# The right half of the expert outputs goes to a table in DRAM by accumulating indirect DMA, the left half stays with put products, and the up product uses two banks

## The reference: an attention layer, then a mixture of experts

```
scores = sigmoid(t @ w_router);  top 8 of 64 experts per token, gates g
for each block (expert e, up to 128 of its tokens toks, gates gs):
    xb  = t[toks]
    out = (silu(xb @ w1[e]) * (xb @ w3[e])) @ w2[e] * gs
routed = sum of the blocks' rows by token        # 256 tokens x 1024
x = x + gate2 * (routed + shared expert(t))
```

## Time and profile before

| | us |
|---|---|
| median of 3 runs (lowest to highest) | 1110.96 (1106.64 to 1120.57) |
| the profiled execution | 1107.02 |
| its span | 1105.2 |
| TensorE busy | 1012.0 |
| VectorE busy | 801.0 |
| ScalarE busy | 583.5 |
| GpSimd busy | 203.6 |

### The profile page before, as it was taken

The page is one execution under the profiler, slowest core; times in us unless marked ns, Lnnn a source line. Parts: engine busy times, 40 slices in busy tenths (PEclk is TensorE's granted clock), DMA queues, the critical chain, the costliest instruction groups (busy, mean ns, idle before and its releaser), DMA issues. The chain is left out here.

```text
span 1105.2 us, 15988 instructions
## 1 busy us (share of the span) xinstructions
PE 1012.0 (92%) x4922; PEld 809.8 (73%) x4922; DVE 801.0 (72%) x1334; ACT 583.5 (53%) x887; POOL 203.6 (18%) x235
## 2 busy tenths in 40 slices
PE   5999999997999898878879688899999999999994
PEld 4778878786776675567668577677888888888883
DVE  4677887666754443466596654799999999999995
ACT  4555554434434332335335321677777777777772
POOL 4142220001000000021130000423223233232230
PEclk9999999998999898988899798999999999999997
DMA  9776776648535242534334212988888888888882
GB/s 320 262 265 220 256 239 226 220 161 274 197 96 173 90 153 77 192 97 153 125 104 153 77 38 102 355 306 344 317 317 345 307 341 334 312 343 318 329 337 79
DMA packets 91203, 247.35 MB, mean 224 GB/s; under 512 B 13244, under 2 KB 23925, under 8 KB 77842
## 3 DMA queue, kind: packets, MB, share of 16 engines
q1 hardware_dynamic: 84578, 226.36, 57.3%
q0 software_dynamic: 6000, 19.96, 4.7%
q10 hardware_dynamic: 576, 0.41, 0.1%
HBM read 244.27 MB, written 2.29 MB: 223 GB/s over the span
## 5 line engine op out<-in xcount | busy, mean ns | idle before, releaser
L1716 PE MATMUL bank<-w_hi,a_hi 128*128 128x512 f32 (+2 forms) x512 | 211.0, 412 | 17.8 <-issue 6.4
L1716 PE MATMUL bank<-w_lo,a_hi 128*128 128x512 f32 (+2 forms) x512 | 202.7, 396 | 0.0
L1716 PE MATMUL bank<-w_hi,a_lo 128*128 128x512 f32 (+2 forms) x512 | 202.5, 395 | 0.0
L1195 DVE TENSOR_TENSOR w_lo<-ring,w_hi 128x1024 fp32r<-128x1024 f32 (+2 forms) x136 | 156.9, 1180 | 62.0 <-ACT w_hi L916 57.5
L916 ACT ACTIVATE w_hi<-ring 128x1024 fp32r<-128x1024 f32 (+2 forms) x140 | 141.3, 1024 | 97.1 <-PE bank L1716 92.2
L1585 DVE TENSOR_TENSOR up_lo<-raw_weights,up_hi 128x1024 fp32r<-128x1024 f32 x136 | 164.4, 1250 | 3.0
L1716 PEld LDWEIGHTS bank<-w_hi,a_hi 128*128 128x128 f32 x512 | 101.0, 197 | 48.7 <-issue 21.9
L1076 ACT ACTIVATE up_hi<-raw_weights 128x1024 fp32r<-128x1024 f32 x136 | 135.8, 1050 | 0.0
L1716 PEld LDWEIGHTS bank<-w_hi,a_lo 128*128 128x128 f32 x512 | 100.8, 197 | 20.7
L771 POOL TENSOR_SCALAR mean_squares<-mean_squares 128x8 f32<-128x8 f32 (+2 forms) x32 | 10.0, 313 | 571.6 <-ACT logits L878 306.3
L1716 PEld LDWEIGHTS bank<-w_lo,a_hi 128*128 128x128 f32 x512 | 101.3, 198 | 19.0 <-issue 1.0
(11 more groups left out here) (257 smaller groups left out, 1824.9 us busy)
## 6 DMA issues: line engine op xcount, KB each, us to landing
raw_weights<-in_w_dram SPq DMA_DIRECT2D x102, 1024.0 KB, 6.9
ring<-in_w_in_dram SPq DMA_DIRECT2D x58, 1024.0 KB, 5.3
merged<-in_w_ada_dram SPq DMA_DIRECT2D x96, 256.0 KB, 5.3
ring<-in_w_out_dram SPq DMA_DIRECT2D x8, 1024.0 KB, 5.2
ring<-in_w_branch_dram SPq DMA_DIRECT2D x6, 1024.0 KB, 4.8
bias<-rel_rows SPq DMA_DIRECT2D x40, 128.0 KB, 5.1
block_rows<-place_rows SPq DMA_DIRECT2D x34, 128.0 KB, 8.6
ring<-in_ws_dram SPq DMA_DIRECT2D x2, 1024.0 KB, 6.0
```

The source lines that it names most:

```text
L1195: dve.tensor_tensor(w_parts[1][:, 2 * p:2 * p + 2, 0:w], view(JOB[it[1:3]], kind)[:, 2 * p:2 * p + 2, :], w_parts[0][:, 2 * p:2 * p + 2, 0 ...
L1716: mm = pe.matmul(ps[:, 0:w], a_parts[za][:, k, t * P:(t + 1) * P], w_parts[zw][:, k, 0:w], start=start, stop=stop)
```

## The change

1. **Right half of the output by DMA.** `y_b[1]` times the gate goes to a new tile `y_add`, without a split. A new table `routed_rows` in DRAM (384 x 512) gets its rows by an indirect DMA that adds (`add_rows`). GpSimd issues it; it waits for `y_gated`. Slots without a token point to row 256 + slot. ScalarE waits for the previous add before it writes `y_add` again. GpSimd clears the table before the routing. SP reads the table back at the end.
2. **Left half by put products.** `scatter` has four matmuls and not eight, once a block; `y_hi` and `y_lo` are half as wide.
3. **`put` without place rows.** GpSimd makes it with two instructions from the token numbers; the row of places, its DRAM tensor and its load are gone.
4. **The second half of `down_lo` on GpSimd**, at the head of its body. The gather follows it, then `put`, the `pick` of block i + 3 and the add.
5. **The up product in two banks**, `bank[4]` and `bank[1]` in turn. `bank[1]` held the shared expert's right half for the first tokens, and so VectorE adds the shared right half to `x` before the loop. The first 3 of 24 up matmuls of a block now stand ahead of the previous block's down product, and the token product stands in the up product after 6 of 8 steps.
6. **The gather skips** slots whose row number is 256 or more.

```diff
-        place_rows = nc.dram_tensor("place_rows", (NV, TOK), F32, kind="Internal").ap()
+        routed_rows = nc.dram_tensor("routed_rows", (TOK + P, CH), F32, kind="Internal").ap()
...
+            return (bank[4], bank[1])[r % 2]
...
+            sp.wait_ge(S("rows_added"), 16 * n_work + ADDED_FROM)
+            sp.dma_start(routed[:, :, :], routed_rows[0:TOK, :].rearrange("(t p) n -> p t n", p=P)).then_inc(S("routed_loaded"), 16)
...
+                    bank_taken(gp, USE["out2", 1, 1])
...
+                    for z in range(NT + 1):
+                        gp.dma_start(routed_rows[z * P:(z + 1) * P, :], xg[:, z % 2, 0:CH]).then_inc(S("rows_added"), 16)
...
             def gather_rows(i, r):
 
...
                 gp.indirect_dma_start(out=xg[:, r % 2, :], out_offset=None, in_=h2_rows,
-                                      in_offset=bass.IndirectOffsetOnAxis(ap=tok[:, r, 0:1], axis=0))\
+                                      in_offset=bass.IndirectOffsetOnAxis(ap=tok[:, r, 0:1], axis=0),
+                                      bounds_check=TOK - 1, oob_is_err=False)\
                   .then_inc(S(f"rows_gathered_{r}"), 16)
+
+            def add_rows(i, r):
+
+                gp.wait_ge(S("y_gated"), i + 1)
+                gp.sem_inc(S("pool_begun"), 1)
+                gp.indirect_dma_start(out=routed_rows, out_offset=bass.IndirectOffsetOnAxis(ap=tok[:, r, 0:1], axis=0),
+                                      in_=y_add[:, :], in_offset=None, compute_op=ALU.add)\
+                  .then_inc(S("rows_added"), 16)
 
...
                     i = m4 * BODY + r
                     with gp.If(n_work > i):
                         after = (r + 2) % BODY
-                        make_pick(i + 2, after, m4 + 1 + (r + 2) // BODY)
-
-                        gp.wait_ge(S("consts_loaded"), 16)
+                        gp.wait_ge(S("down_hi"), 2 * i + 2)
+                        gp.sem_inc(S("pool_begun"), 1)
+                        gp.tensor_tensor(down_lo[:, 1, :], raw[:, 1 - r % 2][:, UP + DM:UP + 2 * DM],
+                                         down_hi[:, 1, :].bitcast(F32), ALU.subtract).then_inc(S("down_lo_1"), 1)
+                        gather_rows(i + 2, after)
+
+                        gp.wait_ge(S("tokens_ready"), i + 1)
                         gp.wait_ge(S("block_done"), i + 1)
-                        gp.wait_ge(S(f"row_loaded_{r}"), 16 * (m4 + 1))
                         gp.sem_inc(S("pool_begun"), 1)
-                        gp.tensor_scalar(put[:, :], row4[:, r, :], consts[:, C_COL:C_COL + 1], None, ALU.is_equal)\
-                          .then_inc(S("put_ready"), 1)
-                        gather_rows(i + 2, after)
+                        for t in range(NT):
+                            gp.tensor_scalar(put[:, t * P:(t + 1) * P], consts[:, C_IOTA:C_IOTA + P], tokf[:, r, 0:1],
+                                             float(-P * t), ALU.subtract, ALU.is_equal).then_inc(S("put_ready"), 1)
+                        make_pick(i + 3, (r + 3) % BODY, m4 + 1 + (r + 3) // BODY)
+                        add_rows(i, r)
...
-                        for hf in range(2):
-
-                            act.wait_ge(S(f"down_{hf}"), i + 1)
-                            act.activation(y_hi[:, hf * CH:(hf + 1) * CH], y_b[hf][:, :], ACT.Copy, scale=gcol[:, r, 0:1])\
-                               .then_inc(S(f"y_hi_{hf}"), 1)
+                        act.wait_ge(S("down_0"), i + 1)
+                        act.activation(y_hi[:, :], y_b[0][:, :], ACT.Copy, scale=gcol[:, r, 0:1]).then_inc(S("y_hi"), 1)
+
+                        act.wait_ge(S("rows_added"), 16 * i + ADDED_FROM)
+                        act.wait_ge(S("down_1"), i + 1)
+                        act.activation(y_add[:, :], y_b[1][:, :], ACT.Copy, scale=gcol[:, r, 0:1]).then_inc(S("y_gated"), 1)
...
+            def take_tokens(i, r, found):
 
                 dve.wait_ge(S("tokens_product"), i + 1)
...
+                dve.tensor_scalar(tok[:, r, :], found[:, 2:3], NO_TOKEN, consts[:, C_NONE:C_NONE + 1], ALU.add, ALU.min)\
+                   .then_inc(S("tokens_ready"), 1)
...
+            dve.wait_ge(S("block_done"), 1)
+            for t in range(NT):
+                dve.tensor_tensor(qn[:, t, :], acc_b[2 * t + 1][:, :], gate_bc[:, 1, CH:DM], ALU.mult)\
+                   .then_inc(S("shared_gated"), 1)
+                dve.wait_ge(S("shared_gated"), t + 1)
+                dve.tensor_tensor(x[:, t, CH:DM], x[:, t, CH:DM], qn[:, t, :], ALU.add).then_inc(S("shared_added"), 1)
...
-                        for f in range(FT):
-                            dve.wait_ge(S("down_hi"), 2 * i + f + 1)
-                            dve.tensor_tensor(down_lo[:, f, :], raw[:, 1 - r % 2][:, UP + f * DM:UP + (f + 1) * DM],
-                                              down_hi[:, f, :].bitcast(F32), ALU.subtract).then_inc(S("down_lo"), 1)
+                        dve.wait_ge(S("down_hi"), 2 * i + 1)
+                        dve.tensor_tensor(down_lo[:, 0, :], raw[:, 1 - r % 2][:, UP:UP + DM],
+                                          down_hi[:, 0, :].bitcast(F32), ALU.subtract).then_inc(S("down_lo_0"), 1)
                         for m in range(2):
                             rest_of_up_weights(i + 1, nxt, 0, m)
+                        take_tokens(i + 2, (r + 2) % BODY, found_b)
                         dve.wait_ge(S("silu_done"), i + 1)
...
-            def scatter(hf, n):
-
-                pe.wait_ge(S(f"y_lo_{hf}"), n)
+            def scatter(n):
+
+                pe.wait_ge(S("put_ready"), NT * n)
+                pe.wait_ge(S("y_lo"), n)
                 for t in range(NT):
                     for part in (y_hi, y_lo):
-                        mm = pe.matmul(acc_b[2 * t + hf][:, :], put[:, t * P:(t + 1) * P],
-                                       part[:, hf * CH:hf * CH + CH], start=False, stop=False, skip_group_check=True)
-                return mm
+                        mm = pe.matmul(acc_b[2 * t][:, :], put[:, t * P:(t + 1) * P], part[:, :],
+                                       start=False, stop=False, skip_group_check=True)
+                mm.then_inc(S("block_done"), 1)
 
...
+            def expert_block(i, r, nxt_loads):
+
+                nxt = (r + 1) % BODY
                 first = isinstance(i, int)
+                pe.wait_ge(S("tokens_ready"), i + 2)
+                up_steps(i, r, range(0 if first else 1, 6))
+                find_tokens(i + 2, (r + 2) % BODY, found_b)
+                up_steps(i, r, range(6, KT))
                 if not first:
-                    for hf in range(2):
-                        pe.wait_ge(S(f"y_lo_{hf}"), i)
+                    pe.wait_ge(S("y_lo"), i)
+                    pe.wait_ge(S("y_gated"), i)
                 turn_rows(nxt, nxt_loads)
                 if not first:
-                    pe.wait_ge(S("put_ready"), i)
-                    scatter(0, i)
+                    scatter(i)
                 pe.wait_ge(S("h_done"), i + 1)
                 for f in range(FT):
 
                     mm = pe.transpose(turned_b[:, f * P:(f + 1) * P], he[:, f:ED:FT], ident)
                 mm.then_inc(S("h_turned"), 1)
-                if not first:
-                    scatter(1, i).then_inc(S("block_done"), 1)
-                find_tokens(i + 2, (r + 2) % BODY)
+                if first:
+                    pe.wait_ge(S("shared_added"), NT)
+                up_steps(i + 1, nxt, range(1))
                 pe.wait_ge(S("h_hi_ready"), i + 1)
-                pe.wait_ge(S("down_lo"), 2 * i + 2)
...
```

More of the change, by code:

```diff
@@ L445, in build @@
         early.close()
-        y_hi = sb("y_hi", [P, DM], F32R, operands)
-        y_lo = sb("y_lo", [P, DM], F32R, operands)
+        y_hi = sb("y_hi", [P, CH], F32R, operands)
+        y_lo = sb("y_lo", [P, CH], F32R, operands)
+        y_add = sb("y_add", [P, CH], F32, operands)
+        sb("rows_end", [P, CH], F32, operands)
         h2 = sb("h2", [P, NT, DM], F32, operands)
@@ L477, in build @@
         ranks = sb("ranks", [P, NT, NV], F32, routing)
-        prow = sb("prow", [NV, TOK], F32, routing)
         gsum = sb("gsum", [P, NT], F32, routing)
@@ L742, in _ @@
                     else:
-                        sp.wait_ge(S("down_lo"), 2 * (r - 1))
+                        for f in range(FT):
+                            sp.wait_ge(S(f"down_lo_{f}"), r - 1)
                         e = load_up(r, r)
                     load_down(r, e)
-                    load_places(r, r)
+                    load_columns(r + 3, (r + 3) % BODY)
             with sp.Fori(1, -(-(MAX_WORK + 1) // BODY)) as m:
@@ L1595, in _ @@
             shared_h(0)
-            take_tokens(0, 0)
+            take_tokens(0, 0, hidden(0))
             shared_h(1)
-            take_tokens(1, 1)
+            take_tokens(1, 1, hidden(0))
             for kh in range(2):
@@ L1917, in _ @@
             pe.wait_ge(S("ranks_ready"), NT)
-            for t in range(NT):
```

(6 more changed lines are left out.)

109 lines of the change are left out of this document (57 added, 52 removed).

## The result

The changed kernel takes **1184.03 us** (median of 4 runs, 1174.06 to 1190.05) where the kernel before takes 1109.1 beside it: ratio **1.0645**, 95% interval 1.0539 to 1.0751. It is slower, as forecast, by about twice the amount forecast (36 us), and outside the range. The profiled execution has a span of 1184.0 us, 78.8 more than that of before (1105.2).

A forecast was written before the change was run, and what follows sets the result against it. TensorE bound the kernel at 11.59 us a block; the ScalarE-VectorE loop with GpSimd's hold would take 12.69. 32 x 1.10 = +35.2, +2.7, -1.9 make +36.0 on 1107.0: 1143.0, forecast 1145, range 1108 to 1170.

The forecast's parts named there:

- The next loop: ScalarE weights, VectorE `up_lo`, tokens, `hT`, `x_block_lo`, three up matmuls, down product: 10.96 us uncontended, 12.69 with GpSimd's hold.
- The hold on `up_lo`: VectorE's two-input `up_lo` stands still while GpSimd subtracts, until +5.34; the pair then runs to +7.62.
- Rival 3: GpSimd's subtraction holds VectorE only partially, as with `put`: 10.96 to 12.69 us a block, 1088 to 1143; 12%.
- 1: The hold does not bite VectorE: a block takes 10.96 us, 1088 in all; 9%.
- 2: TensorE's own work stays the bound: 32 x -0.93 + 0.8 gives 1078, faster by 3%; 6%.
- GpSimd's start: GpSimd's subtraction starts at +2.93 after VectorE's `down_lo`, the add's step being over, and ends at +5.34.
- The small instructions: GpSimd's `put` and `pick` hold VectorE up by 0.2 us; held fully, a block would grow 0.45 more.
- From `x_block_lo` to the end of the down product: On TensorE, three early up matmuls of 0.70 us, then the down product of 2.88, ending at +12.69.
- The clock: TensorE's clock stays at 1.00; a fall, sharing a 5% case, would cost 3.6 us more a block.
- The add's landing: ScalarE's next `y_add`, some 11.9 us after the add's issue, finds it landed in time; estimate 2.6 us.
- 4: GpSimd's subtraction comes late, behind VectorE's first `up_lo`: 1167; full hold by small instructions (1159) included; 10%.
- 5: The add lands after over 11.9 us, each microsecond beyond costing one per block, or the clock falls; 5%.

The follow-up runs named there:

- third experiment: Changed kernel without the adding DMA and ScalarE's wait for it, so the right half lacks the routed experts: 1149.2 us, ratio 1.0308.
- first experiment: Changed kernel with the second half of `down_lo` back on VectorE instead of GpSimd: 1110.88 us, ratio 1.0002.
- second experiment: Changed kernel with each `put` made by one comparison instead of a subtraction and a comparison: 1185.07 us, ratio 1.0676.
- the fifth: Changed kernel with six unread matmuls into an unused bank after the put products, where TensorE idled: 1165.92 us, ratio 1.0529.
- ninth experiment: Changed kernel with the next block's `down_lo` half ahead of the adding DMA on GpSimd, not behind it: 1257.91 us, ratio 1.1232.
- 7: The further version of the changed kernel, but with the adding DMA writing all 128 slots instead of skipping empty ones: 1099.23 us, ratio 0.9891.
- 8: The further version of the changed kernel without the adding DMA, so the right half lacks the routed experts: 1102.89 us, ratio 0.9947.
- the fourth: Kernel before, with the right half's put products left out, so that half lacks the routed experts: 1107.46 us, ratio 0.9945.
- 6: Changed kernel with `down_lo` on VectorE, one up bank, split put products, earlier token product, late shared half, add skipping empty slots: 1099.92 us, ratio 0.99.

## Why the prediction was wrong

The direction, the loop and the hold held; **the size of the loop term failed**: 1.10 us a block forecast, 2.07 measured. The step that failed most is the clock, which the sum has at nothing; next come the start of GpSimd's subtraction and the matmuls behind `x_block_lo`. By its own steps:

- **The next loop** was right in every member and order. Without the add it measured 12.57 for 12.69 (third experiment), of which some is luck, as said there.
- **The hold on `up_lo`** was right as a full hold: 4.31 and 3.83 us for 2.36, and all gone in the first experiment. Rival 3, a partial hold, is out, and so are 1 and 2.
- **GpSimd's start** was the first mis-sized term, +0.35 us a block. I had the add's step begin at +0.8 and take 1.38 us. It begins at +1.62 and takes 1.63, so it reaches +3.25, past the +2.93 at which I had the subtraction start; 3.25 + 2.41 is +5.66, and it ended at +5.69 for +5.34. "If narrowly" was where the text should have worked out the other case. What I lacked is the time between `y_add` and the step: in 12 of the 33 blocks GpSimd sat idle before the add for 1.4 to 2.0 us, and there too the step mostly begins 1.51 us after `y_add` does. What fills the 0.8 us after `y_add` is written stays open.
- **The small instructions** I let hold and be held by 0.2 us, from the earlier trace rows, where `put` and `up_lo` met by their ends. Here the second `put` takes 2.39 us, but that delays the add by 0.1 us at most; the second experiment, with 0.1 us less of `put`, has the same blocks. The Trainium skill, "SBUF — State Buffer", section "SBUF: two separate sides", has it that whichever of the two starts first keeps the pair for the whole instruction. The 2.39 us of the second `put` agree with that; the first `put`, which started first and did not hold the `up_lo` beside it (1.23 us), does not, and the measurement decides.
- **From `x_block_lo` to the end of the down product**, 3.93 us (863.21 to 867.14) for 0.70 + 2.88: +0.35, since the three early matmuls start from a stopped pipeline (0.12 until the first, and 0.97 for the three). The other terms came out 0.27 shorter together. 12.69 + 0.35 + 0.35 - 0.27 = 13.12, what a full-clock block measures: 14 of the missing us.
- **The clock** was the largest miss: the sum has it at nothing, and it cost some 18 us (0.56 us x 32; 0.60 with the one long block). I put its fall at a few per cent, because TensorE's idle time would be "nearer 2 us" than 5.81. It was 1.8, and that was enough; 1.24 in the third experiment was not, and the fifth gained some 15 us by filling it. No row of before had idle pieces of that size once a block, so nothing allowed me to rule it out, and a price at half clock stood in the text (3.6 us a block if all of it, from 0.47 us a matmul; they start 0.43 us apart, which makes it 2.9).
- **The add's landing** in time: right, 4.9 us of the 11.9 allowed. The figure of the Trainium skill ("DMA: Bandwidth & Descriptors", section "Anatomy of one DMA — SWDGE (gpsimd) path"), by which I estimated 2.6 us here, was short by 2.3 in the change and by 8.1 in the ninth experiment; the measurement decides.
- **Block 0** +3.0 for +2.7, **the end** -3.3 for -1.9: right, in sign and about in size.
- **The start**: the 7.75 us ahead of the router are not the change's. The router starts at 659.0 to 660 in the traces of before and of experiments 2, 5, 7 and 8, and at 667.4 to 668.0 in those of the change and of experiments 1, 3, 4, 6 and 9, and the fourth runs before's own code up to there. So it comes in two levels from execution to execution. My sum was made on an execution at the lower level.
- **From the router to the first up matmul**, +4.7, for which the sum has nothing: some 3 us are not the change's either. In six traces (the change, 1, 3, 6, 7 and 9) this stretch has a granted clock of 0.82 and takes 47.2 to 47.7 us, in five (before, 2, 4, 5 and 8) 0.88 to 0.89 and 42.7 to 44.6, and 2 and 5, the change's own code up to there, took 44.6 and 44.1. So 1.1 to 1.6 us are left for the change; TensorE waits 1.54 for the gather there. Why the clock differs stays open.
- **The chances**: forecast, 4, 5 and a fifth of 3 add up to 0.75 for slower, not 0.73, and most of 3 with half of 1 to 0.14, not 0.16.

## What to carry to other kernels

Before an operation goes to GpSimd, lay the two-input instructions of VectorE and all of GpSimd's on one time axis, with the time from a tile being written to the descriptor step that waits for it as a term of its own (0.8 us here). Let a long GpSimd instruction hold VectorE's two-input ones to its end: an engine that is second in busy time can lose more this way (1.95 us a block here) than the move takes off it (1.22). When a change makes the busiest engine idle for a piece of every block, price its clock as a case of its own, not as a mishap. Ask what a transfer's landing will collide with when its issue moves: the same add landed in 4.9 us and, issued 3.7 us later after its `y_add`, in 10.7. And before taking work out of the busiest engine, see what that work covers: four matmuls of 0.93 us hid a wait of 0.54.

## What the hardware showed that was not expected

- **More matmuls, less time**: idle pieces of 1.8 us a block go with stretches at the lower of the two clock levels (a matmul of 128x512 every 0.43 us for 0.233: the down product, of which a part lies in such a stretch, 3.61 us for 2.79); pieces of 1.24 and of 0.41 us do not. Filling them made the kernel some 15 us faster.
- GpSimd's subtraction, recorded from 869.96, overlaps the descriptor step before it (868.76 + 1.63 = 870.39) and takes 2.87 us; without a step before it, 2.41. Its end less 2.41 us is the step's end: the record begins before the work can.
- The step of an indirect DMA on GpSimd begins 0.8 us after the tile that it waits for is written, also when GpSimd is idle.
- A `put` of 0.74 us, begun 0.24 us before VectorE's two-input pair, neither holds nor is held; the next one lasts 2.39 and ends 0.5 us after the pair.
- The same accumulating DMA of 128 rows lands in 4.9 or 10.7 us.
